# Attention's normalization moved into the transposes: a diagonal matrix in place of the identity, and values ahead of transposes in TensorE's order

## The chip, the cores and the metric

The kernel runs on one core of one Trainium2 chip. The metric is the device time of one execution in microseconds (us), lower is better. The engines are named as in the profile: PE (TensorE), DVE (VectorE), ACT (ScalarE), POOL (GpSimd), SP (SyncE, which issues DMAs).

## The reference, cut to what matters

Two layers over 512 latent and 256 context tokens of width 1024. Each layer is a mixer and a SwiGLU feed-forward network, with norms and modulation around both. The change touches the attention in both mixers.

```python
# layer 0, 8 query heads of width 64, 2 key/value heads; latent and context queries
p = softmax(concat([s_loc, s_ctx, sink_l], axis=-1))        # the sink is one more logit per head
o = p[..., :nk] @ v_band + p[..., nk:nk + L] @ v_ctx         # and has no value
# layer 1, 16 heads, latent queries only; s_loc has a relative-position bias
p = softmax(concat([s_loc, s_ctx], axis=-1))
o = p_loc @ v_seg + p_ctx @ v_ctx
```

A softmax row is exp(s - m) / sum. In both versions of the kernel the exps are taken first and the division comes later; the change is in where.

## The kernel before, in words

Each engine has one instruction stream, written out by hand, and waits on semaphores; `claim` and `read_by` on PE keep the eight PSUM banks apart. Around attention, products run in three passes of rounded operands (a high part and a low part, `h_hi` and `h_lo`), with weights split by ACT (`w_hi`, L830) and POOL (`w_lo`, L518).

Attention works in pairs of heads. Layer 0 has 24 pairs: six query tiles of 128 tokens, four pairs each. The tiles in order have 4, 5, 5, 4, 2 and 2 blocks of 128 keys. Layer 1 has 32 pairs of 4 blocks. Two pairs are a chunk, which fills one 128x256 output. For pair p:

- PE `scores(p)` (L1867) writes both heads' scores to PSUM.
- DVE `maximum(p)` (L1329, L1334, L1337) adds mask or bias, writes `prob` (two buffers, by p % 2) and the row maxima, and then the negated maximum `negm`.
- ACT `softmax(p)` (L930) takes the exps of the two heads in place, with the row sums in `rowsum`.
- PE `turns(p)` (L1888, fifth blocks L1895) transposes every 128x128 block of `prob` against the identity, head x = 0 into bank 4 and x = 1 into bank 5; fifth blocks go to bank 4 once it has been read.
- ACT `evacuate(p)` (L919, fifth blocks L922) copies x = 0, DVE `evacuate(p)` (L1347) copies x = 1.
- PE `values(p)` (L1923) multiplies with the values into bank 6 or 7.
- Per chunk: DVE inverts the row sums (L1356, L1365, L1368; in layer 0 with the sink's exp from ACT, L965); PE `norms` (L1935) spreads the inverses over the output's layout with four matmuls; ACT `inverse_rows` (L938) copies them to SBUF; DVE `normalize` (L1374) multiplies; ACT `high` (L945, L949) and DVE `low` (L1383, L1388) split the result into `h_hi` and `h_lo`.

PE's order in step p is scores(p), turns(p-1), values(p-2), and norms in odd steps. ACT's is evacuate(p-1), inverse rows, softmax(p), high. DVE's is maximum(p), the inverse, evacuate(p-1), normalize or low.

POOL takes no part in layer 0's attention. Just ahead of it POOL copies and splits the GLA heads' output (L732, L734), six tiles. In layer 1 POOL adds the relative bias and the mask for pair p (L781), once DVE has read that of pair p-1; in the first four steps it copies a mixed value tile (L792), and in steps 2, 4 and 6 it makes the low part of one weight unit of the output product (L518).

The output products `out0L` and `out1L` (L1716) begin when the last chunk's low part is there. The gate row `gate_b` for layer 1's post-norm is loaded by an ACT DMA during the query and key projection (`gate_load(act, 2)`, L1137).

```python
                for p in range(n_pairs + 2):                       # PE, before
                    if p == 0:
                        start(lambda: scores(0))
                    elif p < n_pairs:
                        scores(p)
                    if 1 <= p <= n_pairs:
                        turns(p - 1)
                    if p >= 2:
                        values(p - 2)
                        if p % 2 == 1:
                            norms(p // 2 - 1)
```

## Time and profile before

| | |
|---|---|
| Time, median of 3 runs (lowest to highest) | 1751.51 us (1749.96 to 1753.03) |
| The profiled execution's own time | 1752.69 us |
| Its span, first to last instruction | 1750.9 us |
| Mean granted PE clock | 0.987 |
| PE busy | 1667.4 us, 95% |
| DVE, ACT, POOL busy | 708.4, 644.1, 676.9 us |
| Layer 0's attention, first transposes to the output product | 275.3 to 358.2 us |
| Layer 1's attention, first transposes to the output product | 1201.7 to 1314.7 us |

Positions are microseconds from the start of the span. A row of the timeline has the start, the length, the engine, the line, the operation with its operands, the count of records merged, and in brackets the engine's idle time before it with what ended it. Matmul ends are modelled and matmuls overlap, so PE's progress is read from the starts.

### The profile page before, as it was taken

Reading aid. Unit: us, or ns where it says so; the run is one execution under the profiler, and the core shown is the slowest. Engines: PE = TensorE matmul, PEld = TensorE weight load, DVE = VectorE, ACT = ScalarE, POOL = GpSimd, SP = SyncE. Lnnn points to the kernel's source line nnn. Section 1 sums busy time; section 2 is a strip of 40 time slices with the busy share of each in tenths; the row PEclk is TensorE's granted clock in tenths of the full one; section 3 lists DMA queues with packets and bytes.
Section 4 is the critical chain, followed back from the end, with each engine's and each line's share of the span. In section 5 each row is a group of like instructions: output and inputs, shape, how many; then the busy total and the mean of one; then the engine's idle time right before and its main releaser. Section 6 shows DMA issues by size and latency. Waiting matters only on the chain.

```text
span 1750.9 us, 25757 instructions
## 1 busy us (share of the span) xinstructions
PE 1667.4 (95%) x10178; PEld 1387.9 (79%) x10178; DVE 708.4 (40%) x1121; ACT 644.1 (37%) x1120; POOL 676.9 (39%) x456
## 2 busy tenths in 40 slices
PE   5999998999999999999899999999999899999997
PEld 2868886777877888878899878877887788888886
DVE  3335456717588735402555420005771551011103
ACT  4242215727422122213555343235772522222222
POOL 2212222038554544443542043334443444444443
PEclk9999999999999999999999999999999899999999
DMA  8643111023466746533556645433002353333331
GB/s 325 212 150 99 42 25 49 2 73 108 145 193 193 230 143 188 167 91 109 145 169 183 193 117 113 92 94 101 2 2 60 100 165 95 105 90 98 96 98 69
DMA packets 210131, 207.17 MB, mean 118 GB/s; under 512 B 16454, under 2 KB 180828, under 8 KB 209756
## 3 DMA queue, kind: packets, MB, share of 16 engines
q1 hardware_dynamic: 197352, 165.53, 31.7%
q10 hardware_dynamic: 12660, 39.99, 7.4%
q8 instruction: 82, 1.34, 0.3%
q14 instruction: 37, 0.30, 0.1%
HBM read 203.37 MB, written 2.13 MB: 117 GB/s over the span
## 4 chain that ended last, share of the span: by engine, by line
PE 82%; DVE 5%; issue 4%; POOL 3%; ACT 3%; DMA 2%; SPq 0%; ACTq 0%; POOLq 0%; DVEq 0%
PE ps L1689 39%; PE ps L1716 29%; PE ps L1867 3%; PE ps L1923 3%; PE ps L1888 3%; POOL w_lo L518 3%; DMA mod_early<-in_w_mod 1%; ACT w_hi L830 1%; PE ps L1763 1%; PE ps L1802 1%; DVE xs L1278 1%; PE ps L1935 1%; PE ps L2051 1%; DVE full L1227 1%; DMA w_raw<-in_w_ffn_in 1%
## 5 line engine op out<-in xcount | busy, mean ns | idle before, releaser
L518 POOL TENSOR_TENSOR w_lo<-w_raw,w_hi 128x1024 fp32r<-128x1024 f32 (+1 forms) x223 | 557.5, 2502 | 896.3 <-ACT w_hi L830 896.1
L1689 PE MATMUL ps<-h_hi,w_hi 128*128 128x512 f32 (+1 forms) x1488 | 496.7, 352 | 11.7 <-POOL w_lo L518 8.0
L1689 PE MATMUL ps<-h_hi,w_lo 128*128 128x512 f32 (+1 forms) x1488 | 492.0, 349 | 0.0
L1689 PE MATMUL ps<-h_lo,w_hi 128*128 128x512 f32 (+1 forms) x1488 | 491.0, 348 | 0.0
L830 ACT ACTIVATE w_hi<-w_raw 128x1024 fp32r<-128x1024 f32 (+1 forms) x275 | 287.2, 1046 | 354.2 <-PE ps L1716 342.8
L1689 PEld LDWEIGHTS ps<-h_hi,w_hi 128*128 128x128 f32 x1488 | 270.0, 189 | 56.6 <-issue 20.2
L1689 PEld LDWEIGHTS ps<-h_hi,w_lo 128*128 128x128 f32 x1488 | 269.8, 189 | 36.2
L1689 PEld LDWEIGHTS ps<-h_lo,w_hi 128*128 128x128 f32 x1488 | 269.8, 189 | 36.0
L518 DVE TENSOR_TENSOR w_lo<-w_raw,w_hi 128x1024 fp32r<-128x1024 f32 x52 | 69.2, 1332 | 200.5 <-ACT w_hi L830 197.5
L1716 PE MATMUL ps<-w_hi,hid_hi 128*128 128x512 f32 x440 | 136.7, 392 | 8.0 <-ACT mod_row L842 4.2
L1297 DVE TENSOR_TENSOR hid_f<-silu_g,ps 128x512 f32<-128x512 f32 (+1 forms) x66 | 39.3, 595 | 255.3 <-PE ps L1689 254.9
L1716 PE MATMUL ps<-w_hi,hid_lo 128*128 128x512 f32 x440 | 136.1, 391 | 0.0
L1716 PE MATMUL ps<-w_lo,hid_hi 128*128 128x512 f32 x440 | 135.9, 390 | 0.0
L901 ACT ACTIVATE hid_hi<-hid_f 128x512 fp32r<-128x512 f32 (+1 forms) x66 | 37.0, 561 | 252.9 <-DVE hid_f L1297 252.9
L1716 PE MATMUL ps<-w_hi,h_hi 128*128 128x512 f32 (+1 forms) x352 | 106.4, 384 | 13.8 <-POOL w_lo L518 3.5
L1716 PE MATMUL ps<-w_lo,h_hi 128*128 128x512 f32 (+1 forms) x352 | 105.4, 382 | 0.0
L1716 PE MATMUL ps<-w_hi,h_lo 128*128 128x512 f32 (+1 forms) x352 | 104.8, 379 | 0.0
L1716 PEld LDWEIGHTS ps<-w_hi,hid_hi 128*128 128x128 f32 x440 | 82.7, 189 | 27.2 <-issue 10.3
L1716 PEld LDWEIGHTS ps<-w_lo,hid_hi 128*128 128x128 f32 x440 | 82.9, 188 | 17.4
L1716 PEld LDWEIGHTS ps<-w_hi,hid_lo 128*128 128x128 f32 x440 | 82.9, 188 | 17.3
L1716 PEld LDWEIGHTS ps<-w_hi,h_hi 128*128 128x128 f32 x352 | 66.5, 192 | 28.2 <-issue 7.1
L897 ACT ACTIVATE silu_g<-ps 128x512 f32<-128x512 f32 (+1 forms) x66 | 34.6, 524 | 145.8 <-PE ps L1689 145.6
(213 smaller groups left out, 1790.4 us busy)
## 6 DMA issues: line engine op xcount, KB each, us to landing
w_raw<-in_w_ffn_in SPq DMA_DIRECT2D x132, 512.0 KB, 3.8
w_raw<-in_w_ffn_out SPq DMA_DIRECT2D x66, 512.0 KB, 3.5
mod_raw<-in_w_mod ACTq DMA_DIRECT2D x42, 512.0 KB, 4.5
w_raw<-in_na_w_in SPq DMA_DIRECT2D x32, 512.0 KB, 3.7
mod_early<-in_w_mod SPq DMA_DIRECT2D x30, 512.0 KB, 9.0
full<-in_w_mod ACTq DMA_DIRECT2D x15, 512.0 KB, 4.9
w_raw<-in_ab_w_in SPq DMA_DIRECT2D x9, 512.0 KB, 4.6
w_raw<-in_ab_w_in SPq DMA_DIRECT2D x16, 256.0 KB, 3.8
```

What stands on the lines that cost most here:

```text
L518: eng.tensor_tensor(w_lo[:, u % RING, 0:width], w_raw[:, u % RAW, 0:width], w_hi[:, u % RING, 0:width].bitcast(F32), ALU.subtract).then_in ...
L830: act.activation(w_hi[:, u % RING, 0:width], w_raw[:, u % RAW, 0:width], ACT.Copy).then_inc(w_hi_done, 1)
L897: act.activation(silu_g[:, f % 2, 0:width], ps(2 * (f % 2), 0, width), ACT.Silu)\
L901: act.activation(hid_hi[:, j * width:(j + 1) * width], hid_f[:, f % 2, 0:width], ACT.Copy)\
L1227: dve.scalar_tensor_tensor(post_place(name, i), src, rs_post[:, n:n + 1], gate_b[:, lc, :], ALU.mult, ALU.mult).then_inc(post_n, 1)
L1278: dve.scalar_tensor_tensor(acc, mod_place(m), c, acc, ALU.mult, ALU.add).then_inc(mod_acc, 1)
L1297: dve.tensor_tensor(hid_f[:, f % 2, 0:width], silu_g[:, f % 2, 0:width], ps(2 * (f % 2) + 1, 0, width), ALU.mult).then_inc(ff_full, 1)
L1689: mm = pe.matmul(o[0], sta(x, o), mov(y, o), start=first and n == 0, stop=last and n == 2)
L1716: mm = pe.matmul(o, act(x, k, t), w[y][:, c:c + n], start=k == 0 and (x, y) == ("hi", "hi") and first_in_bank(name, i, c), stop=k == n_uni ...
L1867: mm = pe.matmul(ps(scores_bank(layer, p, x), at, at + width), q, kk[:, col:col + width], start=at % 512 == 0, stop=i == len(runs[x]) - 1, ...
L1888: mm = pe.transpose(ps(4 + x, j * P, (j + 1) * P), probs(p, x, j), ident[:])
L1923: mm = pe.matmul(ps(bank, at, at + P, 64 * x, 64 * x + 64), value_tile(p, x, j), turned_probs(layer, p)[:, x, j * P:(j + 1) * P], start=j ...
```

## The change

It does six things.

1. `turns` becomes a matmul of each block of `prob` with a diagonal matrix of the inverse row sums, one 128x128 diagonal per head, so that the transposed block comes out normalized. It waits for that diagonal once per pair.
2. POOL makes the diagonals, `scale(layer, p)`: a power of -1 on the two row sums, then the identity times the inverse, broadcast, 128x256. There is one buffer for them, so `scale(p)` also waits for the turns of p-1.
3. The sink becomes a column of `prob` in layer 0, written by POOL (`sink_column`), so that the exp's row sum holds it.
4. `norms`, `inverse_rows`, `normalize`, the shift and the inverse on DVE are gone; `high` and `low` read PSUM directly.
5. PE's order in step p becomes scores(p), values(p-2), turns(p-1). `prob` has three buffers, and `maximum(p)` waits for the turns of p-3.
6. `gate_load(act, 2)` moves behind layer 1's attention, since the third prob buffer takes `gate_b`'s place.

```diff
@@ POOL, ahead of feed(sp("out0C")), after the copies of the GLA output
+            feed(sp("out0L") + 1)
+            def sink_column(p):
+                f = PAIRS[0][p][2]
+                if p >= 3:
+                    pool.wait_ge(at_p, 2 * (p - 2))
+                pool.tensor_scalar(prob0[:, p % 3, :, 0:1].rearrange("p x n -> p (x n)"), sink[:, f:f + 5:4], 1.0 / SCALE,
+                                   None, ALU.mult).then_inc(at_sink, 1)
+            def scale(layer, p):
+                q = PAIR0[layer] + p
+                n = CHUNK0[layer] + p // 2
+                pool.wait_ge(at_p, 2 * (q + 1))
+                if p:
+                    pool.wait_ge(at_ta, q)
+                    pool.wait_ge(at_tb, q)
+                    if fifths(layer, p - 1):
+                        pool.wait_ge(at_t5, fifths(layer, p - 1))
+                rows, inv = (x[:, 2 * (p % 2):2 * (p % 2) + 2] for x in (rowsum[:, n % 2, :], sm[:, n % 2, 3, :]))
+                pool.tensor_tensor(inv, rows, one_hot[:, 34:36], ALU.pow).then_inc(at_rinv, 1)
+                pool.wait_ge(at_rinv, q + 1)
+                one = ident[:]
+                one = bass.AP(one.tensor, one.offset, [list(one.ap[0]), [0, 2], [1, P]])
+                pool.tensor_tensor(scale_of(layer), one, bcast(inv, P), ALU.mult).then_inc(at_scale, 1)
+            for p in range(3):
+                sink_column(p)
+            for p in range(len(PAIRS[0])):
+                scale(0, p)
+                if p + 3 < len(PAIRS[0]):
+                    sink_column(p + 3)
@@ POOL, layer 1, at the end of the loop over pairs that adds the bias
+                if p:
+                    scale(1, p - 1)
+            scale(1, len(PAIRS[1]) - 1)
@@ ACT attention
-                for p in range(n_pairs + 3):
+                for p in range(n_pairs + 2):
+                    if p % 2 == 1 and p >= 3:
+                        high((p - 3) // 2)
                     if 1 <= p <= n_pairs:
                         evacuate(p - 1)
-                    if p % 2 == 0 and p >= 4:
-                        inverse_rows(p // 2 - 2)
                     if p < n_pairs:
                         softmax(p)
@@ ACT
-                    if i == 6:
-                        gate_load(act, 2)
...
             attention(1, lambda: layer1_values("v1C", C_TILES))
+            act.wait_ge(at_p, 2 * (PAIR0[1] + len(PAIRS[1])))
+            act.wait_ge(at_ta, PAIR0[1] + len(PAIRS[1]))
+            act.wait_ge(at_tb, PAIR0[1] + len(PAIRS[1]))
+            gate_load(act, 2)
@@ DVE attention
-                for p in range(n_pairs + 4):
+                for p in range(n_pairs + 2):
                     if p < n_pairs:
                         maximum(p)
-                        if p % 2 == 1 and layer == 0:
-                            shift(p // 2)
-                    if p % 2 == 0 and 2 <= p <= n_pairs:
-                        inverse(p // 2 - 1)
+                    if p % 2 == 1 and p >= 3:
+                        low((p - 3) // 2)
                     if 1 <= p <= n_pairs:
                         evacuate(p - 1)
-                    if p % 2 == 0 and p >= 4 and p // 2 - 2 < n_pairs // 2:
-                        normalize(p // 2 - 2)
-                    if p % 2 == 1 and p >= 5:
-                        low(p // 2 - 2)
@@ PE attention
                 def turns(p):
                     n = s_cols(layer, p) // P
+                    pe.wait_ge(at_scale, q0 + p + 1)
                     for x in range(2):
-                        pe.wait_ge(at_p, 2 * (q0 + p) + x + 1)
                         claim(4 + x)
                         for j in range(min(n, 4)):
-                            mm = pe.transpose(ps(4 + x, j * P, (j + 1) * P), probs(p, x, j), ident[:])
+                            mm = pe.matmul(ps(4 + x, j * P, (j + 1) * P), probs(p, x, j), scale_of(layer)[:, x, :],
+                                           start=True, stop=True)
...
                     elif p < n_pairs:
                         scores(p)
+                    if 2 <= p <= n_pairs + 1:
+                        values(p - 2)
                     if 1 <= p <= n_pairs:
                         turns(p - 1)
-                    if p >= 2:
-                        values(p - 2)
-                        if p % 2 == 1:
-                            norms(p // 2 - 1)
```

## Rows read from the trace of the kernel before

**Rows 1.** The page: engines over the span, and the chain by engine.
```profile
PE 1667.4 (95%) x10178; PEld 1387.9 (79%) x10178; DVE 708.4 (40%) x1121; ACT 644.1 (37%) x1120; POOL 676.9 (39%) x456
...
PE 82%; DVE 5%; issue 4%; POOL 3%; ACT 3%; DMA 2%; SPq 0%; ACTq 0%; POOLq 0%; DVEq 0%
```

**Rows 2.** Timeline of layer 1's attention, two steps (start, length, engine, line, operation).
```profile
1228.26 1.09 PE L1888 MATMUL ps<-ident,prob 128*128 128x128 f32 x8
...
1228.95 0.60 ACT L919 ACTIVATE prob_t<-ps 128x512 f32<-128x512 f32 x1 [0.86 <-PE ps L1888]
...
1229.29 0.44 PE L1923 MATMUL ps<-prob_t,c_v 128*64 128x128 f32 x4
...
1229.45 0.38 ACT L938 ACTIVATE on<-ps 128x256 f32<-128x256 f32 x1
...
1230.24 0.72 ACT L930 ACTIVATE prob<-prob,negm 128x512 f32<-128x512 f32 x1 [0.41 <-DVE negm L1337]
...
1231.48 1.09 PE L1888 MATMUL ps<-ident,prob 128*128 128x128 f32 x8
...
1231.58 0.19 ACT L930 ACTIVATION_READ_ACCUMULATOR prob<-prob,negm 128x1 f32 x1
...
1235.14 1.09 PE L1888 MATMUL ps<-ident,prob 128*128 128x128 f32 x8
```

**Rows 3.** An fp32 matmul's records (timeline), and the transposes of layer 1 (groups by form).
```profile
195.12 1.95 PE L2051 MATMUL ps<-b_v,att_m 128*128 128x128 f32 x16
...
L1888 PE MATMUL ps<-ident,prob 128*128 128x128 f32 x256 | 36.0, 284 | 2.5 <-ACT prob L930 2.4
```

**Rows 4.** Groups by form on POOL (count, busy us, mean ns of one, idle before).
```profile
L781 POOL TENSOR_TENSOR bias_m<-rel,near_b 128x256 f32<-128x256 f32 x16 | 10.6, 682 | 25.5 <-DVE raw_max L1329 25.5
...
L792 POOL COPY x_res<-c_v 64x1024 f32<-64x1024 f32 x4 | 4.1, 1035 | 12.7 <-ACT c_v L1144 12.3
```

**Rows 5.** POOL's power, line 712 (min/median/max ns, first and last start).
```profile
L712 POOL TENSOR_TENSOR rs_pre<-ms_pre,half_neg x22: 550/551/1622, 15.1 to 1369.8; 128x1 f32<-128x1 f32 x22
...
L712 POOL TENSOR_TENSOR gla_rs<-gla_ms,half_neg x6: 1007/1010/1018, 200.1 to 265.4; 128x4 f32<-128x4 f32 x6
```

**Rows 6.** Timeline of ACT in layer 0, a step of five blocks.
```profile
299.82 0.60 ACT L919 ACTIVATE rope<-ps 128x512 f32<-128x512 f32 x1 [0.54 <-PE ps L1888]
...
301.23 0.82 ACT L930 ACTIVATE prob<-prob,negm 128x640 f32<-128x640 f32 x1
...
302.76 0.19 ACT L930 ACTIVATION_READ_ACCUMULATOR prob<-prob,negm 128x1 f32 x1
```

**Rows 7.** Groups by form in layer 0's attention: the exp of two blocks.
```profile
L930 ACT ACTIVATE prob<-prob,negm 128x256 f32<-128x256 f32 x16 | 8.0, 502 | 1.2 <-DVE negm L1334 0.9
```

**Rows 8.** Timeline at the start and the end of layer 0's attention.
```profile
275.34 1.97 PE L1888 MATMUL ps<-ident,prob 128*128 128x128 f32 x8 [0.89 <-ACT prob L930]
...
278.88 1.27 POOL L734 TENSOR_TENSOR h_lo<-b_o,h_hi 128x512 fp32r<-128x512 f32 x1
...
353.45 0.87 PE L1888 MATMUL ps<-ident,prob 128*128 128x128 f32 x4
...
358.22 0.70 PE L1716 MATMUL ps<-w_hi,h_hi 128*128 128x512 f32 x2 [2.24 <-DVE h_lo L1383]
```

**Rows 9.** Timeline at the start and the end of layer 1's attention.
```profile
1202.83 2.36 POOL L518 TENSOR_TENSOR w_lo<-w_raw,w_hi 128x1024 fp32r<-128x1024 f32 x1 [4.43 <-ACT w_hi L830]
...
1206.11 1.87 PE L1888 MATMUL ps<-ident,prob 128*128 128x128 f32 x8 [2.27 <-ACT prob L930]
...
1308.67 1.36 PE L1888 MATMUL ps<-ident,prob 128*128 128x128 f32 x8 [0.17 <-ACT prob L930]
...
1314.72 0.70 PE L1716 MATMUL ps<-w_hi,h_hi 128*128 128x512 f32 x2 [2.28 <-DVE h_lo L1388]
```

**Rows 10.** Windows (stretch, us, busy PE PEld DVE ACT POOL, PE clock, DMA share, GB/s).
```profile
275.00:281.00 6.00, 5.66 (x24) 4.33 (x24) 4.00 (x13) 3.69 (x11) 4.92 (x5) 0.50 0.46 133
840.00:860.00 20.00, 15.75 (x126) 15.03 (x125) 9.69 (x14) 10.98 (x18) 9.52 (x7) 1.00 0.46 134
```

More of the change, by code:

```diff
@@ L274, in build @@
         with ExitStack() as early:
-            sb("before", [P, D], scope=early)
+            prob1_c = sb("prob1_c", [P, 2, 4 * P], scope=early)
             rel = sb("rel", [P, 2, 8, BIAS_RUN], scope=early)
-            on1 = sb("on1", [P, 2 * P], scope=early)
+            scale1 = sb("scale1", [P, 2, P], scope=early)
         with ExitStack() as early:
@@ L338, in build @@
             a_q = sb("a_q", [P, 4, TOK], scope=s1)
+            with ExitStack() as s2:
+                prob0 = sb("prob0", [P, 3, 2, 1 + 5 * P], scope=s2)
             qg = sb("qg", [P, 4, TOK], scope=s1)
-            with ExitStack() as s2:
-                prob0 = sb("prob0", [P, 2, 2, 5 * P], scope=s2)
             kg = sb("kg", [P, 4, TOK], scope=s1)
@@ L624, in scores_bank, with prob_of, scale_of @@
             return 2 * x if layer == 0 else 2 * x + p % 2
-        def mixed_out(layer):
-            return full[:, 0:2, :].rearrange("p k n -> p (k n)") if layer == 0 else on1[:]
+        def prob_of(layer, p, x):
+            if layer == 0:
+                return prob0[:, p % 3, x]
+            return prob1_c[:, x] if p % 3 == 2 else prob1[:, p % 3, x]
+        def scale_of(layer):
+            return full[:, 0:2, :] if layer == 0 else scale1[:]
         block = ctx.enter_context(nc.Block())
@@ L911, in attention @@
                 pairs, q0, c0 = PAIRS[layer], PAIR0[layer], CHUNK0[layer]
-                prob = (prob0, prob1)[layer]
                 def evacuate(p):
@@ L961, in attention @@
                         meanwhile()
-                    if p % 2 == 1 and p < n_pairs and layer == 0:
-                        c = c0 + p // 2
-                        act.wait_ge(at_shift, c + 1)
-                        act.activation(sm[:, c % 2, 1, :], sm[:, c % 2, 0, :], ACT.Exp).then_inc(at_sink, 1)
-                    if p % 2 == 0 and p >= 4:
-                        high(p // 2 - 2)
             act.dma_start(x_res[:, 0:LT, :], a["x"][0].rearrange("(t p) d -> p t d", p=P)).then_inc(x_in, 16)
@@ L1310, in attention @@
                 pairs, q0, c0 = PAIRS[layer], PAIR0[layer], CHUNK0[layer]
-                prob = (prob0, prob1)[layer]
                 def maximum(p):
@@ L1316, in maximum @@
                     t, g, f = pairs[p]
[L1317 to L1321 removed]
+                    if p >= 3:
+                        dve.wait_ge(at_ta, q0 + p - 2)
+                        dve.wait_ge(at_tb, q0 + p - 2)
+                        if fifths(layer, p - 3):
+                            dve.wait_ge(at_t5, fifths(layer, p - 3))
                     for x in range(2):
@@ L1328, in maximum @@
                             added = bias_m[:, 2 * P * x:2 * P * x + n]
-                        dve.tensor_tensor_reduce(prob[:, s, x, 0:n], ps(scores_bank(layer, p, x), 0, n), added, 1.0,
+                        at = int(layer == 0)
+                        dve.tensor_tensor_reduce(prob_of(layer, p, x)[:, at:at + n], ps(scores_bank(layer, p, x), 0, n), added, 1.0,
                                                  -3.0e38, ALU.add, ALU.max, raw_max[:, s, x:x + 1]).then_inc(at_r, 1)
@@ L1773, in modulation_sum @@
                 claim(bank)
[L1774 removed]
+                pe.wait_ge(small_done, 5)
                 pe.wait_ge(mod_acc, sums_done(KT * (b + 1) - 1))
@@ L1848, in attention @@
                 pairs, q0, c0 = PAIRS[layer], PAIR0[layer], CHUNK0[layer]
-                prob = (prob0, prob1)[layer]
                 def scores(p):
@@ L1894, in turns @@
                         for x in range(2):
-                            mm = pe.transpose(ps(4, x * P, (x + 1) * P), probs(p, x, 4), ident[:])
+                            mm = pe.matmul(ps(4, x * P, (x + 1) * P), probs(p, x, 4), scale_of(layer)[:, x, :],
+                                           start=True, stop=True)
                         mm.then_inc(at_t5, 1)
@@ L1927, in values @@
                                 mm.then_inc(at_o, 1)
-                def norms(c):
-                    bank = 6 + (c0 + c) % 2
-                    pe.wait_ge(at_rinv, c0 + c + 1)
-                    for i in range(2):
-                        for x in range(2):
-                            r = sm[:, (c0 + c) % 2, 3, 2 * i + x:2 * i + x + 1]
-                            mm = pe.matmul(ps(bank, (2 + i) * P, (3 + i) * P, 64 * x, 64 * x + 64),
-                                           bass.AP(r.tensor, r.offset, [list(r.ap[0]), [0, 64]]), ident[:],
-                                           start=True, stop=True, skip_group_check=True)
-                            mm.then_inc(at_rr, 1)
-                    read_by((bank,), (at_on, c0 + c + 1))
+                    if p % 2 == 1:
+                        read_by((bank,), (at_lo, c0 + p // 2 + 1))
                 n_pairs = len(pairs)
```

56 lines of the change are left out of this document (12 added, 44 removed).

## The prediction

> **What bounds the kernel now.** The page comes first: its engine row and its chain [rows 1]. The reader is to see that PE is busy 95% of the span and holds 82% of the chain that ended last, so PE time is kernel time almost everywhere, and that the other engines, under 41% each, have room on average. An average says nothing of a stage, so the second view is the timeline of layer 1's attention, two steps of its steady part [rows 2]. PE works without a gap over 0.2 us: transposes at 1228.26, values at 1229.29, the next transposes at 1231.48, the ones after at 1235.14. A step without norms is 3.22 us, one with norms 3.66 us. The norms cost 0.44 us of PE per chunk and nothing else separates the two steps. ScalarE's evacuation, exps and sums go on beside this.
>
> **What is removed from PE.** Four norm matmuls per chunk of two pairs, 0.44 us each chunk [rows 2]. There are 16 chunks in layer 1 and 12 in layer 0: 7.0 + 5.3 = 12.3 us if PE stays the bound. With them go four DVE operations and two or three of ScalarE per chunk; they lie beside PE in the steady part and are priced at nothing, except at the two tails, below.
>
> **The transposes become products.** A transpose is one record of the trace: 8 per pair, 32 pairs, 256 records [rows 3]. They take 0.86 us per pair, 0.107 each, since values start 1.03 us after them of which 0.17 is issue. An fp32 matmul of the same full width, 128x128 on 128 columns, is two records: the eight of one tile are 16 records, whose starts run over 1.95 - 0.27 = 1.68 us in 15 intervals, 0.111 apart [rows 3]. So I take 0.222 us for each product with the diagonal, against 0.107. A pair of four blocks goes from 0.86 to 1.78 us, +0.92. By PE alone a layer 1 step is 3.22 + 0.92 = 4.14 us against a mean of 3.44: already slower, norms or not. The ends are 0.107 (should the product be one record) and, upward, 0.25.
>
> The rule that speaks against this more strongly: the Trainium skill, "TensorE: Matmul & The Clock Gate", section Terms, calls the transpose mode 4x faster for FP32 than what it replaces. By it a product would take four times 0.107, 0.43 us. The fp32 rows of this kernel say 0.222, and the sum goes by them.
>
> **The order closes a loop.** This is the main term. Transposes of p-1 now wait for the diagonal of p-1 (both exps, then two POOL operations), and ScalarE does evacuate(p-1), then softmax(p), in that order, while evacuate(p-1) waits for the transposes of p-1. So each step contains one full round: transposes(p-1), evacuation, two exps, POOL, transposes(p). Its length, from rows 2 for four blocks:
> - transposes to the evacuation's start: 0.69 now (1228.26 to 1228.95), with four records of half x=0. Eight records add 4 x 0.111 + 0.03: 1.16.
> - evacuation, until ScalarE's next operation: 0.50 (1228.95 to 1229.45).
> - both exps and their sums: 1230.24 to 1231.58 + 0.19 = 1.53.
> - POOL: the power and the diagonal of 128x256. The diagonal's nearest row is the bias add of the same size, 0.68 [rows 4]. The power of 128x1 is 0.55 and of 128x4 1.01 [rows 5], so 128x2 by the line between them is 0.70. Three hand-overs are some 0.25, by the 0.10 between the modelled end of the fourth transpose (0.32 + 0.27 after the first's start) and the evacuation. Together 1.63.
>
> The sum is 4.82 us per step, more than PE's 4.14, so the loop sets the step and not PE. Before, the same round needed no POOL, one exp fewer ahead of the first half, and eight records fewer: it fitted into 3.22 us. DVE is not in it: its maxima of p start when scores(p) are out, which the new order leaves early, and evacuate of x=1 ends about 2.75 us into the round, ahead of the values.
>
> For layer 0 the blocks vary. Five blocks: the evacuation's start to the softmax is 1.41 (299.82 to 301.23), because the fifth blocks are turned between; their two transposes become four records, +0.22; the exps take 302.76 + 0.19 - 301.23 = 1.72 [rows 6]. Round: 1.16 + 1.63 + 1.72 + 1.63 = 6.14 us. Two blocks: an exp is 0.50 [rows 7], the pair of them with sums 1.10, the evacuation half of the above, the first half four records (0.70): 0.70 + 0.28 + 1.10 + 1.63 = 3.71 us.
>
> **Layer 0's sum.** From the first transposes to the last there are 23 rounds. Three of four blocks 14.5, the change to five 5.0, seven of five 43.0, the change back 5.95, three of four 14.5, the change to two 4.4, seven of two 26.0: 113.2 us. Now it is 353.45 - 275.34 = 78.1 [rows 8]. So +35.1. The start: POOL reaches its sink columns only after its copies of GLA output, which end at 278.88 + 1.27 = 280.15 [rows 8], and the softmax waits for them. First transposes: 280.15 + 0.3 + 1.53 + 1.63 = 283.6 against 275.34, +8.3. Tail: the last transposes (0.89), DVE's evacuation, eight value records, high, low, first product: about 3.5 against 4.77, -1.3.
>
> **Layer 1's sum.** POOL's queue ahead of diagonal 1: w_lo to 1202.83 + 2.36 = 1205.19, two bias adds 1.36, the copy of v_mix 1.04 [rows 4, 9], then 1.63: 1209.2 against 1206.11, +3.1. The same queue (2.36 + 1.36 + 1.63, a little more where a bias comes in four adds) outlasts two later rounds by about 0.7 each, +1.4. Thirty rounds of 4.82 are 144.6 against 1308.67 - 1206.11 = 102.6 [rows 9], +42.0. Tail: 1.78 for the products, then evacuation, values, high, low: 5.4 against 6.05, -0.6.
>
> **The clock.** While POOL holds the start PE idles; now after such an idle the granted clock was 0.50, the 1.2 GHz level, for 275 to 281 [rows 10]. At it a half's eight records take 0.9 us more. I add 2 us for two rounds in layer 0, 0.9 in layer 1 and 1 for the stage of two blocks, where PE will be busy under half the time. In the rest PE idles about 1 us a round; a stretch with PE busy 15.75 of 20 us kept 1.00 [rows 10].
>
> **Other edits.** The load of gate 2 moves behind layer 1's attention; its reader is the post-norm, which has the whole output product ahead of it and so hides it (uncovered, one load would be late once). A third prob buffer loosens maximum(p), which bound nothing. The sink column adds one column to 128x640. POOL's sink operations stand behind scale(p), inside the round's slack. POOL's prefetched w_lo of the output product is as far as ScalarE allows, as now. All nothing.
>
> Total: layer 0 +35.1 + 8.3 - 1.3 + 3 = +45.1; layer 1 +3.1 + 1.4 + 42.0 - 0.6 + 0.9 = +46.8. Together +92. The profiled execution took 1752.69 us, 1.2 above the median of 1751.51; against the median that is 1843 us.
>
> **Rivals.**
> 1. PE's own sum binds, because POOL or the hand-overs are quicker than I price, or ScalarE overlaps more. A round then is near PE's: 0.65 less over 54 rounds, -35: 1808. For it: 4.14 and 4.82 are close, and a power of 0.55 takes 0.15 off. Against: both POOL operations have rows of their kind. 15%.
> 2. The clock does not hold in layer 0. At 1.2 GHz a round of five blocks would be PE's doubled sum, some 9.4 us; for half of layer 0's rounds that is about +25: 1868. For it: idle of 1 to 1.6 us in every round, never seen here in a row. Against: at the low clock PE has no idle left, and rows 10. 12%.
> 3. The product costs four times a transpose. The first half adds 0.8 us to each round, and layer 1 becomes PE's, near 6.0: about +56 more, 1900. Rows 3 speak against it. The Trainium skill's 4x would give this. 3%.
> 4. Not slower: the products run as one record each and POOL's two operations hide, the norms' 12.3 us go, the start costs 8.3 + 3.1 and the tails give 1.9: about -3, 1749. It decides where the round falls under 3.22 us. Without POOL it would be 0.69 + 0.50 + 1.53 = 2.72, so POOL would have to take 0.5; the power alone has 0.55 at the least. 3%. The 5% left lie between it and rival 1, 2 of them near the time of now.
>
> **Range and chances.** The forecast has 62%, with a range of its own of 1825 to 1865: the power's ends are -0.15 and +0.31 on 54 rounds (-8, +17), the diagonal -0.05 to +0.1, the hand-overs 0.1 either way. Rivals 1 and 2 with theirs bring it to 1800 to 1880. A measurement of this kernel can tell about 0.2% from no change. Rival 4 and those 2 make faster 0.02 and same 0.03; all else is slower, 0.95.
>
> **What would show it.** In the profile after: 16 matmul records per pair of four blocks where 8 transposes were, some 0.11 apart; layer 1's transposes repeating every 4.8 us, five-block ones every 6.1; PE waiting in them for POOL's diagonal, 0.5 to 1.3 us a step; the power near 0.70 and the diagonal near 0.68; ScalarE waiting for PE before each evacuation; the first transposes of layer 0 near 283.6. Steps near 4.1 us with no wait for POOL would make rival 1 right, a granted clock under 0.9 over the attention stages rival 2, and steps under 3.4 us the whole reading wrong.

## The result and the profile after

The changed kernel takes 1839.44 us, the median of 4 runs (1837.74 to 1843.27), against 1752.06 (1749.96 to 1753.03) for the kernel before in the same session: 1.0508 times as long, with a 95% interval of 1.0491 to 1.0525. The forecast was 1843 us. The profiled execution spans 1837.9 us, 87.0 more than before. Line numbers below are those of the changed kernel: its transposes are now the products of L1885 (fifth blocks L1893), scores L1864, values L1922, the products of the output projection L1714; POOL's power is L762 and its diagonal L766.

The page of the kernel after, engines and chain, against [rows 1]:

```profile
PE 1707.9 (93%) x10386; PEld 1430.9 (78%) x10386; DVE 703.9 (38%) x1041; ACT 631.7 (34%) x1080; POOL 755.0 (41%) x593
...
PE 76%; POOL 8%; ACT 6%; issue 5%; DVE 4%; DMA 1%; SPq 0%; ACTq 0%; POOLq 0%; DVEq 0%
```

PE is busy 40.5 us more, which is less than half of what the span grew by. The rest shows in the chain: PE falls from 82% to 76%, POOL rises from 3% to 8% and ScalarE from 3% to 6%. Engines that had little part in the chain now carry more of it.

A steady round of layer 1, from the timeline (start, length, engine, line, operation, count, idle before and releaser), against [rows 2]:

```profile
1292.57 2.05 PE L1885 MATMUL ps<-scale,prob 128*128 128x128 f32 x16 [0.48 <-POOL scale L766]
...
1293.77 0.60 ACT L959 ACTIVATE prob_t<-ps 128x512 f32<-128x512 f32 x1 [2.73 <-PE ps L1885]
1294.26 0.71 ACT L972 ACTIVATE prob<-prob,negm 128x512 f32<-128x512 f32 x1
...
1295.58 0.19 ACT L972 ACTIVATION_READ_ACCUMULATOR prob<-prob,negm 128x1 f32 x1
...
1295.85 0.71 POOL L762 TENSOR_TENSOR sm<-rowsum,one_hot 128x2 f32<-128x2 f32 x1 [1.76 <-ACT prob L972]
...
1296.63 0.61 POOL L766 TENSOR_TENSOR scale<-ident,sm 128x256 f32<-128x256 f32 x1
...
1297.30 2.05 PE L1885 MATMUL ps<-scale,prob 128*128 128x128 f32 x16 [0.48 <-POOL scale L766]
```

The reader can walk round it: products to evacuation 1.20, evacuation to exps 0.49, exps and sums 1.51, a hand-over of 0.08, the power and its own hand-over 0.78, the diagonal and the last hand-over 0.67. That is 4.73 us, and no engine is busy all through it: PE waits 0.48, ScalarE 2.73, POOL 1.76. This is how a loop looks in a timeline. Each engine has a gap, each gap names the next engine, and the lengths of one turn add up to the step.

The waits of layer 1's attention, 1250 to 1395 (engine and line, waited for, us in total, times, longest), and POOL's groups over the whole kernel (count, busy us, mean ns of one, idle before), against [rows 4, 5]:

```profile
ACT prob_t L959 <- PE ps L1885: 60.3, 30, 4.5
...
POOL sm L762 <- ACT prob L972: 32.7, 18, 2.1
...
PE ps L1885 <- POOL scale L766: 17.6, 30, 2.1
...
POOL sm L762 <- ACT prob_c L972: 16.3, 9, 2.1
```

```profile
L762 POOL TENSOR_TENSOR sm<-rowsum,one_hot 128x2 f32<-128x2 f32 x56 | 39.7, 710 | 130.7 <-ACT prob L972 114.1 <-ACT prob_c L972 16.3
L766 POOL TENSOR_TENSOR scale<-ident,sm 128x256 f32<-128x256 f32 x32 | 19.7, 614 | 2.5
```

PE waits for the diagonal in all 30 rounds of this stretch, though only for 17.6 us in all. A saving of POOL's time alone would win at most these 17.6 us in this stretch; below that PE's own sum takes over.

In layer 0 a step of five blocks, a step of two, the start and the end, against [rows 6, 8]; the last two rows are the start of layer 1's second round and its end, against [rows 9]:

```profile
277.45 1.26 POOL L741 TENSOR_TENSOR h_lo<-b_o,h_hi 128x512 fp32r<-128x512 f32 x1
278.80 0.82 POOL L749 TENSOR_SCALAR prob<-sink 128x2 f32<-128x2 f32 x3
279.10 1.28 ACT L972 ACT_TABLE_LOAD   x1 [11.64 <-POOL prob L749]
280.40 0.72 ACT L972 ACTIVATE prob<-prob,negm 128x513 f32<-128x513 f32 x1
...
317.05 2.05 PE L1885 MATMUL ps<-full,prob 128*128 128x128 f32 x16 [1.05 <-POOL full L766]
...
323.19 2.05 PE L1885 MATMUL ps<-full,prob 128*128 128x128 f32 x16 [1.05 <-POOL full L766]
...
379.57 1.16 PE L1885 MATMUL ps<-full,prob 128*128 128x128 f32 x8 [1.28 <-POOL full L766]
...
383.21 1.16 PE L1885 MATMUL ps<-full,prob 128*128 128x128 f32 x8 [1.02 <-POOL full L766]
...
402.19 1.19 PE L1714 MATMUL ps<-w_hi,h_hi 128*128 128x512 f32 x2 [1.50 <-DVE h_lo L1387]
...
1252.51 3.45 PE L1885 MATMUL ps<-scale,prob 128*128 128x128 f32 x16 [2.11 <-POOL scale L766]
...
1401.96 0.93 PE L1714 MATMUL ps<-w_hi,h_hi 128*128 128x512 f32 x2 [1.37 <-DVE h_lo L1392]
```

Five blocks take 6.14 us and two blocks 3.64. The first products of layer 0 start at 283.47 and those of the last pair at 397.78, so its rounds take 114.3 us where 78.1 were. The output product of layer 0 starts 43.97 us later than before. Layer 1's attention runs from its first products at 1245.08 to 1401.96, 156.9 us against 113.0 (1201.68 to 1314.72): 43.8 more. The two make 87.8, so everything outside the two stages, the moved load of the gate row included, gives back 0.8 to the 87.0 of the span.

Windows of the kernel after (stretch, us, busy PE PEld DVE ACT POOL, PE clock, DMA share, GB/s), against [rows 10]:

```profile
275.00:281.00 6.00, 0.00 (x0) 0.00 (x0) 0.00 (x0) 1.88 (x2) 4.22 (x7) 0.50 0.27 84
303.00:347.00 44.00, 36.59 (x380) 31.07 (x376) 21.68 (x51) 19.98 (x48) 11.53 (x22) 1.00 0.01 1
370.00:398.00 28.00, 18.26 (x159) 12.96 (x159) 12.19 (x47) 11.79 (x43) 11.67 (x21) 1.00 0.00 1
1250.00:1395.00 145.00, 126.14 (x1284) 110.44 (x1282) 80.75 (x210) 66.99 (x182) 90.05 (x170) 0.99 0.04 12
```

The gaps of 0.5 to 1.3 us in every round leave the granted clock at 0.99 to 1.00, the 2.4 GHz level, even among the steps of two blocks, where PE is busy 18.3 of 28 us.

### The profile page after: what moved, and what is told of

The parts are those of the page before. It is cut to its first block, busy times and chain, and to the rows that moved or that the text cites. A ratio compares the mean times of both kernels' runs of the same rounds, so it can differ in the third digit from the quotient of the medians.

```text
span 1837.9 us, 26165 instructions
## 1 busy us (share of the span) xinstructions
PE 1707.9 (93%) x10386; PEld 1430.9 (78%) x10386; DVE 703.9 (38%) x1041; ACT 631.7 (34%) x1080; POOL 755.0 (41%) x593
## 4 chain that ended last, share of the span: by engine, by line
PE 76%; POOL 8%; ACT 6%; issue 5%; DVE 4%; DMA 1%; SPq 0%; ACTq 0%; POOLq 0%; DVEq 0%
PE ps L1687 39%; PE ps L1714 28%; PE ps L1885 4%; ACT prob L972 3%; POOL w_lo L517 2%; POOL sm L762 2%; DMA mod_early<-in_w_mod 1%; POOL scale L766 1%; ACT w_hi L871 1%; PE ps L1800 1%; PE ps L1761 1%; DVE xs L1310 1%; POOL full L766 1%; ACT prob_c L972 1%; PE ps L2038 1%
## 5 line engine op out<-in xcount | busy, mean ns | idle before, releaser
L1714 PE MATMUL ps<-w_hi,hid_hi 128*128 128x512 f32 x440 | 136.0, 390 | 8.0 <-ACT mod_row L883 4.3
L1714 PE MATMUL ps<-w_lo,hid_hi 128*128 128x512 f32 x440 | 135.5, 389 | 0.0
L1714 PE MATMUL ps<-w_hi,hid_lo 128*128 128x512 f32 x440 | 135.5, 389 | 0.0
L1714 PE MATMUL ps<-w_hi,h_hi 128*128 128x512 f32 (+1 forms) x352 | 107.0, 386 | 11.9 <-POOL w_lo L517 3.2
L1714 PE MATMUL ps<-w_lo,h_hi 128*128 128x512 f32 (+1 forms) x352 | 105.5, 382 | 0.0
L1714 PE MATMUL ps<-w_hi,h_lo 128*128 128x512 f32 (+1 forms) x352 | 105.2, 381 | 0.0
L1714 PEld LDWEIGHTS ps<-w_hi,hid_hi 128*128 128x128 f32 x440 | 82.1, 188 | 27.0 <-issue 10.3
L1714 PEld LDWEIGHTS ps<-w_lo,hid_hi 128*128 128x128 f32 x440 | 82.6, 188 | 17.3
L1714 PEld LDWEIGHTS ps<-w_hi,hid_lo 128*128 128x128 f32 x440 | 82.6, 188 | 17.2
L762 POOL TENSOR_TENSOR sm<-rowsum,one_hot 128x2 f32<-128x2 f32 x56 | 39.7, 710 | 130.7 <-ACT prob L972 114.1
L1714 PEld LDWEIGHTS ps<-w_hi,h_hi 128*128 128x128 f32 x352 | 66.9, 193 | 26.2 <-issue 5.6
```

The lines of the kernel that those rows point to most:

```text
L762: pool.tensor_tensor(inv, rows, one_hot[:, 34:36], ALU.pow).then_inc(at_rinv, 1)
L1714: mm = pe.matmul(o, act(x, k, t), w[y][:, c:c + n], start=k == 0 and (x, y) == ("hi", "hi") and first_in_bank(name, i, c), stop=k == n_uni ...
```

## The experiments

The theory going in: two costs, the products on PE (+0.9 a pair) and a loop through ScalarE and POOL, the longer of which sets the step. The rivals: PE's sum alone, a costlier product, and PE's new order. Each run is compared with the kernel before in its own session, whose median lies between 1748.06 and 1752.06, so a difference of 2 or 3 us between medians of two sessions says nothing by itself; where one matters, the stages are read from the traces. The runs stand in the order of the questions.

**Is it PE's order?** `e1_old_pe_order` turns pair p-1 before it takes the values of p-2, as the kernel before did.

```
@@ ACT: high(c) behind softmax(p); DVE: low(c) behind evacuate(p-1)
@@ PE attention
-                    if 2 <= p <= n_pairs + 1:
-                        values(p - 2)
                     if 1 <= p <= n_pairs:
                         turns(p - 1)
+                    if 2 <= p <= n_pairs + 1:
+                        values(p - 2)
```

> The changed kernel with TensorE's old order (transposes of p-1 ahead of values of p-2); ACT's high and DVE's low go behind the evacuation, since they wait for those values. Theory (the round transposes, ACT evacuation, two exps, POOL power and diagonal, transposes sets the step, and values are not in it): layer 1 stays at 4.73 us a step, five blocks at 6.14, total 1839 within 4 us. Rival (TensorE's new order is what opens the gap): steps fall towards TensorE's own sum of 4.15 us, total about 1805.

Measured: 1836.8 us, ratio 1.0493 (1.0476 to 1.0511). Its products in layer 1 stand at 1262.03 and 1266.75, 4.72 us apart. The medians differ by 2.6 us, which is not clear of the noise (87.4 and 86.2 over the kernel before of each session), and the step is the same in either order. The loop does not need PE's new order. That it needs the other two things, products that wait for POOL and a ScalarE that evacuates p-1 before it takes the exps of p, is for the runs below.

**What do the products cost by themselves?** `e3_before_with_products` is the kernel before with each transpose written as an fp32 matmul with the identity.

```
-   mm = pe.transpose(ps(4 + x, j * P, (j + 1) * P), probs(p, x, j), ident[:])
+   mm = pe.matmul(ps(4 + x, j * P, (j + 1) * P), probs(p, x, j), ident[:], start=True, stop=True)
```

> The kernel before with one part of the change alone: each transpose is an fp32 matmul with the identity. Theory (0.222 us for a product against 0.107 for a transpose, and TensorE is the bound): +0.92 us for each pair of four blocks in layer 1 (+29), in layer 0 +0.92 x 8, +1.15 x 8, +0.46 x 8 (+20, a little less where ACT is waited for): total about 1799. Rival 1 (a product is one record like a transpose): 1752. Rival 2 (a product costs four transposes, 0.43 us): +2.6 us a pair, total above 1880.

Measured: 1792.61 us in a single execution, 42 above the 1750.61 of the kernel before beside it. PE's timeline in layer 1:

```profile
1264.23 2.05 PE L1888 MATMUL ps<-ident,prob 128*128 128x128 f32 x16
...
1268.31 2.05 PE L1888 MATMUL ps<-ident,prob 128*128 128x128 f32 x16
...
1272.83 2.05 PE L1888 MATMUL ps<-ident,prob 128*128 128x128 f32 x16
```

The products are followed by the next operation 1.98 us after their start, where transposes take 1.03 [rows 2]: 0.95 a pair, against 0.92 predicted. The steps are 4.08 us, and 4.52 with norms, where the same pairs took 3.13 and 3.56 before (transposes at 1241.92, 1245.05 and 1248.61; their scores are shorter than those of [rows 2]), and none waits. The Trainium skill ("TensorE: Matmul & The Clock Gate", Terms) has the transpose mode 4x faster for FP32, and doesn't say against what; with the 0.17 of issue taken off both, the rows say 1.81 to 0.86, 2.1 times, and the measurement decides.

**And POOL's wait by itself?** `e4_transposes_wait_for_pool` is the kernel after with plain transposes that still wait for the diagonal. It leaves the normalization out.

```
-   mm = pe.matmul(ps(4 + x, j * P, (j + 1) * P), probs(p, x, j), scale_of(layer)[:, x, :], start=True, stop=True)
+   mm = pe.transpose(ps(4 + x, j * P, (j + 1) * P), probs(p, x, j), ident[:])
```

> The changed kernel with plain transposes against the identity in place of the products, still waiting for POOL's diagonal; the normalization is left out of the output. Theory (only the first half's four extra records lie in the round, the other half's beside it): layer 1 4.73 to 4.26 us, five blocks 6.14 to 5.45, two blocks 3.64 to 3.42: total about 1814. Rival (TensorE's sum is the bound, so all of the doubling comes back): -0.92 us a pair, total about 1791.

Measured: 1812.03 us in a single execution. PE's timeline in layer 1:

```profile
1265.74 1.09 PE L1885 MATMUL ps<-ident,prob 128*128 128x128 f32 x8
...
1269.96 1.09 PE L1885 MATMUL ps<-ident,prob 128*128 128x128 f32 x8 [0.93 <-POOL scale L766]
```

4.22 us a step: the loop without the four products of its first half, 4.73 less some 0.5. PE now idles 0.93 of it.

**The other two corners.** `e8_products_without_pool` keeps after's order and products, but multiplies by the identity and waits for the exps alone. `e11_neither_product_nor_pool` is the same with plain transposes in place of the last line below. Both leave the normalization out.

```
@@ POOL
-                scale(0, p)
...
@@ PE turns
-                    pe.wait_ge(at_scale, q0 + p + 1)
+                    pe.wait_ge(at_p, 2 * (q0 + p + 1))
...
+                            mm = pe.matmul(ps(4 + x, j * P, (j + 1) * P), probs(p, x, j), ident[:], start=True, stop=True)
```

> The changed kernel without POOL's power and diagonal: products with the identity that wait for the two exps alone; the normalization is left out of the output. Theory (POOL's two operations with their hand-overs are 1.5 us of each round, and without them TensorE's own sum binds): layer 1 at 4.2 us, five blocks at about 5.0, two blocks at 2.1 to 2.3, total about 1797. Rival (the round is set by ACT and DVE): total 1825 or more.

> The kernel after with plain transposes, and with POOL's power and diagonal out of the step: the transposes wait for the two exps alone. The normalization is left out, for this is the fourth corner beside the two runs that have the products without POOL (1793.25) and POOL's wait without the products (1812.03). Theory: PE is the bound again, in layer 1 at 3.12 to 3.22 us a step with no step longer, since the norms are out of it: by the 0.44 us of PE per chunk that is -12.3 us against the kernel before; the start of layer 0 keeps its wait for the sink columns (+5 to +6.6), the tails give 1 to 2. Together 1742 to 1746. The corner then says that the products alone cost 49 and POOL's wait alone 68, and that both together cost less than their sum, because one hides in the other. Rival: the two kernels' difference by products is the 41 us measured on the kernel before, so this run gives 1793.25 - 41 = 1752, and taking the norms off PE was worth next to nothing, because ScalarE's order (evacuation, then both exps, now with both exps ahead of every transpose) makes a round as long as PE's sum: then PE waits for prob in each step and steps exceed 3.22 us.

Measured: 1793.25 us in a single execution for the first, with steps of 4.18 and 4.08 us in layer 1 that wait for nothing, 5.02 for five blocks and 2.38 for two. The second takes 1748.23 (10 runs), ratio 0.9986 (0.9975 to 0.9996), which fell between the two numbers expected of it. Its mechanism is the theory's, with steps of 3.12 us and no wait (1249.81, 1252.93, 1256.05 for the transposes of layer 1), so the rival's loop is not there. Its size is not: the start of layer 0 cost more than was allowed for, as PE's and ScalarE's rows there show:

```profile
279.71 1.28 ACT L968 ACT_TABLE_LOAD   x1 [11.63 <-POOL prob L749]
...
282.58 1.97 PE L1881 MATMUL ps<-ident,prob 128*128 128x128 f32 x8 [8.51 <-ACT prob L968]
```

The transposes start 7.2 us later than in [rows 8], in a stage that itself started 0.8 us earlier, so the wait for the sink columns costs 8.0. What taking the norms off PE gives back is therefore about 11.5, the shorter tails with it: 3.5 net and these 8.0. The traces agree: from the first transposes to the output product layer 0 takes 77.9 us instead of 82.9, layer 1 106.3 instead of 113.0. The four corners together:

```
                          transposes   products
waiting for the exps      1748.2       1793.3
waiting for POOL          1812.0       1839.4
```

Products alone cost 45 us, POOL's wait alone 64, both 91 and not 109: some 18 us of either hide in the other. Two of the four are single executions, and each is of another session. The same two stages in the traces, from the first transposes to the output product, give 46, 63 and 91, so the picture holds. This is also why the change can't be mended by making one of the two cheap.

**Can ScalarE's order open the loop?** `e2_softmax_first` lets ScalarE take the exps of p before it evacuates p-1.

```
@@ ACT attention
                 for p in range(n_pairs + 2):
+                    if p < n_pairs:
+                        softmax(p)
                     if p % 2 == 1 and p >= 3:
                         high((p - 3) // 2)
                     if 1 <= p <= n_pairs:
                         evacuate(p - 1)
-                    if p < n_pairs:
-                        softmax(p)
```

> The changed kernel with one order turned on ACT: softmax(p) ahead of evacuate(p-1), so that the exps of p no longer wait for the transposes of p-1. Theory: the round is cut, and TensorE's own sum is next: layer 1 4.73 to 4.15 us a step (-17 us over 30 steps), five blocks 6.14 to about 5.0 (-9), four blocks in layer 0 to 4.0 (-5), two blocks 3.64 to about 2.6, where the single diagonal buffer binds (-8): total about 1800. Rival (POOL's two operations and their hand-overs set the step by themselves): total stays at 1839.

Measured: 1827.39 us, ratio 1.0442 (1.0427 to 1.0458). A miss by 27 us, by the stages in the trace half of it in layer 1 and half in layer 0. PE's timeline and one wait of 1250 to 1380:

```profile
1286.70 0.44 PE L1922 MATMUL ps<-prob_t,c_v 128*64 128x128 f32 x4 [0.82 <-DVE prob_t L1379]
...
1287.72 2.05 PE L1885 MATMUL ps<-scale,prob 128*128 128x128 f32 x16
...
1291.90 2.05 PE L1885 MATMUL ps<-scale,prob 128*128 128x128 f32 x16
...
1296.98 2.05 PE L1885 MATMUL ps<-scale,prob_c 128*128 128x128 f32 x16
```

```profile
DVE h_lo L1392 <- ACT h_hi L985: 26.8, 14, 1.9
```

Every second step is the 4.18 us expected; the others take 5.08. In those ScalarE's high() now stands behind the exps, DVE's low() waits for it, and DVE's own evacuation, which the values need, is queued behind low(). What wasn't counted in layer 1 was the queue behind the instruction that waits. `e5_softmax_first_evacuate_next` puts both evacuations ahead of high() and low().

```
@@ ACT: softmax(p), evacuate(p-1), high
@@ DVE
                         maximum(p)
-                    if p % 2 == 1 and p >= 3:
-                        low((p - 3) // 2)
                     if 1 <= p <= n_pairs:
                         evacuate(p - 1)
+                    if p % 2 == 1 and p >= 3:
+                        low((p - 3) // 2)
```

> The changed kernel with ACT's order softmax(p), evacuate(p-1), high, and DVE's order maximum(p), evacuate(p-1), low. With the softmax first but high and low ahead of the evacuations (e2) layer 1's steps alternated between 4.18 and 5.08 us. Theory (in the long steps DVE's evacuation stood behind low, which waited for ACT's high, which waited for the exps): both steps come to 4.18 us, TensorE's own sum, total about 1814. Rival (something else of odd steps costs 0.9 us): total stays at 1827.

Measured: 1813.4 us, ratio 1.0361 (1.0339 to 1.0383). The step of layer 1:

```profile
1271.51 2.05 PE L1885 MATMUL ps<-scale,prob 128*128 128x128 f32 x16
...
1275.73 1.49 PE L1885 MATMUL ps<-scale,prob_c 128*128 128x128 f32 x11
```

4.22 us with no gap on PE: in layer 1 the loop is open and PE's own sum binds, as rival 1 would have had it. In layer 0 it is not open for five blocks:

```profile
315.52 2.05 PE L1885 MATMUL ps<-full,prob 128*128 128x128 f32 x16
...
318.59 0.71 PE L1893 MATMUL ps<-full,prob 128*128 128x128 f32 x4 [1.02 <-ACT rope L959]
...
321.77 2.05 PE L1885 MATMUL ps<-full,prob 128*128 128x128 f32 x16
```

A step is 6.25 us there, where the changed kernel has 6.14, the first run with the exps first was expected to have 5.0, and the corner without POOL has 5.02. The fifth blocks go to bank 4 and wait for ScalarE's evacuation of it, which now stands behind both exps, and the scores of the next pair stand behind the fifth blocks: the new order opens one loop and closes another. Two blocks take 2.86 (371.03 to 385.33, five steps) against 3.64. The forecast of 1814 came true with this unseen: it lies 14 us above the sum of the run before, and no term of it is named for the difference.

So some 26 of the change's 87 us are ScalarE's order (with DVE's): 10.3 in layer 0 and 16.1 in layer 1 by the two stages in the traces. The change's scheme stays 3.6% slower even so, since the products alone are worth 45 and the five-block steps some 10 more (1.23 each over the corner without POOL, for eight pairs).

**The start of layer 0.** `e7_sinks_before_copies` has POOL write the sink columns first and spread its six copies between the rounds.

```
@@ POOL
             for p in range(3):
                 sink_column(p)
+            for t in range(3):
+                mixed_copy(t)
             for p in range(len(PAIRS[0])):
                 scale(0, p)
...
+                if p + 3 < NT:
+                    mixed_copy(p + 3)
```

> The changed kernel with POOL's sink columns and three of six GLA copies ahead of layer 0's attention, the other copies one each behind diagonals 0 to 2, and ACT waiting for the sink ahead of the maximum. Theory (POOL's copies ahead of the sink hold the start of layer 0's attention, with the exp table load behind that wait): the first transposes 6 us earlier, total about 1832. Rival (the start is hidden, or the copies are only moved): total stays at 1839.

Measured: 1833.21 us (1828.52 to 1836.69), ratio 1.0476 (1.0442 to 1.0509): near the 1832 expected. But against the kernel before of its session it is 85 us longer, the changed kernel 87, and its four runs lie 8 us apart, so the total doesn't settle it. The trace does:

```profile
272.38 1.28 ACT L977 ACT_TABLE_LOAD   x1 [5.23 <-DVE negm L1371]
...
276.74 3.78 PE L1890 MATMUL ps<-full,prob 128*128 128x128 f32 x16 [2.84 <-POOL full L767]
```

The first products start 6.7 us earlier than in the changed kernel (276.74 against 283.47, 0.3 of it because the stage started earlier), and layer 0's output product 6.9 earlier (395.27). So the start's wait is real time, some 6.5 us of it. Part stays, for the table load is still in the way.

**Can the norms leave PE without a product?** The corner without either cost says that plain transposes with the norms off PE are not slower than before. `e6_normalize_in_place` scales prob before plain transposes: DVE takes the reciprocal, POOL multiplies both halves by it, and PE turns p-2 and takes the values of p-3, so that the scaling has a step of its own.

```
@@ POOL
-                pool.tensor_tensor(scale_of(layer), one, bcast(inv, P), ALU.mult).then_inc(at_scale, 1)
+                for x in range(2):
+                    head = 2 * (p % 2) + x
+                    w = prob_of(layer, p, x)[:, at:at + n]
+                    last = pool.tensor_scalar(w, w, sm[:, c % 2, 3, head:head + 1], None, ALU.mult)
+                last.then_inc(at_scale, 1)
@@ PE: scores(p), turns(p-2), values(p-3)
```

> Another place for the division: plain transposes against the identity; DVE takes the reciprocals between its two maxima; POOL multiplies prob in place by them, two operations of 128x512; transposes of p-2 and values of p-3 in step p (three prob buffers do for it), so that the exps and POOL have a step more; the sink columns go ahead of the GLA copies on POOL. Theory (nothing of the round is left on TensorE's path and transposes stay at 0.107 us): the kernel before less the norms' 12.3 us and about 1 us of tails: about 1738, layer 1 at 3.22 us in every step. Rival (POOL, with bias 1.6 and products 1.2 us in each step of 3.22, becomes the bound or DVE waits for it): layer 1 at 3.4 to 3.7 us, total 1745 to 1760.

Measured: 1811.63 us, ratio 1.0349 (1.0328 to 1.037). A miss by 74 us: the rival came true, beyond its own range of 1745 to 1760. POOL's group and the window of layer 1 (columns as above):

```profile
L761 POOL TENSOR_SCALAR prob_c<-prob_c,sm 128x512 f32<-128x512 f32 x20 | 31.1, 1565 | 0.0
```

```profile
1215.00:1370.00 155.00, 105.82 (x1046) 87.30 (x1045) 88.51 (x246) 72.67 (x186) 151.79 (x177) 0.92 0.04 11
```

POOL is busy 151.8 of 155 us: it is the bound, and layer 1's steps are 4.65 us, 1.35 to 1.46 of them PE's wait for POOL. The Trainium skill ("GPSIMD Engine Reference", 4.1 Engine selection) calls POOL's one-input operations roughly line-rate and its two-input ones about 2x slower than VectorE's. Here the one-input form is the slow one: 1565 ns, where the two-input form of the next run takes 1042; the measurement decides.

`e9_in_place_act_and_pool` halves POOL's part: ScalarE scales x=0 by a copy with a scale, POOL x=1 by a tensor-tensor multiply that reads the same column again and again.

```
@@ ACT
+                    act.activation(w, w, ACT.Copy, scale=sm[:, c % 2, 3, 2 * (p % 2):2 * (p % 2) + 1]).then_inc(at_scaled, 1)
@@ POOL
+                inv = bass.AP(inv.tensor, inv.offset, [list(inv.ap[0]), [0, n]])
+                pool.tensor_tensor(w, w, inv, ALU.mult).then_inc(at_scale, 1)
```

> As e6, in place of POOL's two scalings by a per-row scalar, which took 1.57 us for 128x512 and held POOL for 3.1 us of each 4.6 us step: ACT scales head x=0 (a Copy with a scale, 0.50 us of ACT by the evacuation of the same size) and POOL head x=1 as a product of two tensors, 1.27 us by its subtraction of the same size. Theory (POOL's load of bias and scaling sets e6's step, not the pipeline): POOL comes to 1.6 + 1.3 = 2.9 us a step, layer 1 to 3.22 to 3.4 us, total 1737 to 1744, under the kernel before. Rival (the deeper pipeline itself costs, or POOL at 90% of a step is still the bound): layer 1 at 3.6 us or more, total 1752 or more.

Measured: 1747.42 us (11 runs), ratio 0.998 (0.9971 to 0.9989); 4 us under the kernel before beside it and 3 us above what was expected. Its groups by form:

```profile
L763 POOL TENSOR_TENSOR prob<-prob,sm 128x512 f32<-128x512 f32 x30 | 31.2, 1042 | 13.2 <-DVE sm L1358 13.2
L982 ACT ACTIVATE prob<-prob,sm 128x512 f32<-128x512 f32 x30 | 21.5, 715 | 1.1 <-DVE sm L1358 1.1
```

The steady steps are the 3.22 us of the theory (1226.58, 1229.80, 1233.02) and 3.12 further on, without a wait. The excess is at the start of layer 1's attention, where PE waits 1.58 us for POOL (1213.31) and 2.24 for DVE (1222.24) and the granted clock was 0.72 (1202 to 1214).

`e10_in_place_act_and_dve` gives x=1 to DVE, behind its maxima, and leaves POOL out.

```
@@ DVE
+                    dve.tensor_scalar(w, w, sm[:, c % 2, 3, head:head + 1], None, ALU.mult).then_inc(at_scale, 1)
@@ POOL
-                scale(0, p)
```

> As e9, with head x=1 scaled by DVE behind its maximum (0.4 us, by the 0.75 us of its 128x1024 scaling) and POOL out of it. Theory: DVE comes to about 3.05 us and ACT to 2.7 us a step, both under TensorE's 3.22, so layer 1 runs at 3.22 us in every step, layer 0 as before without norms: total about 1738, 12 us under the kernel before. Rival (DVE's queue is too full, or waits for POOL's bias adds where both read SBUF): layer 1 at 3.4 us or more, total 1744 or more.

Measured: 1741.28 us (1738.87 to 1743.2), ratio 0.9941 (0.9929 to 0.9954): 0.6% under the kernel before (10.1 us under the 1751.39 beside it), and 3 us above the forecast for it. PE's timeline in layer 1, the group of DVE's scaling, the end of layer 1, and the same stage in a window:

```profile
1250.47 1.19 PE L1897 MATMUL ps<-ident,prob 128*128 128x128 f32 x8
...
1253.68 1.09 PE L1897 MATMUL ps<-ident,prob 128*128 128x128 f32 x8
...
1304.13 0.70 PE L1726 MATMUL ps<-w_hi,h_hi 128*128 128x512 f32 x2 [1.37 <-DVE h_lo L1400]
```

```profile
L1348 DVE TENSOR_SCALAR prob<-prob,sm 128x512 f32<-128x512 f32 x30 | 21.2, 708 | 0.0
```

```profile
1250.00:1290.00 40.00, 40.00 (x440) 33.37 (x438) 38.77 (x114) 36.34 (x91) 20.62 (x46) 1.00 0.01 2
```

Steps are 3.1 to 3.2 us with PE busy 40 of 40, where every second one was 3.66 [rows 2], or 3.55 in this stretch of the kernel before (1251.73 to 1255.28). The price is that DVE (38.8) and ScalarE (36.3) are nearly full as well: there is little more to be had this way. From the scores of the second pair to the output product, layer 1's attention takes 110.0 us (1194.17 to 1304.13) against 114.1 (1200.62 to 1314.72), and layer 0's 80.3 (272.98 to 353.26) against 84.9 (273.32 to 358.22). These are 8.7 of the 13.1 us between the spans (1737.8 against 1750.9); the other 4.4 lie where the two kernels are the same: 0.3 ahead of layer 0's attention, 1.5 between the two (842.4 against 840.9) and 2.5 behind layer 1's (436.2 against 433.7), where the granted clock of the first 85 us was 0.96 against 0.92. That last part goes with the clock and is not shown to belong to the edit.

## Why the prediction was right

Right in sign, in size to 3.6 us, and in mechanism, step by step:

- *Four norm matmuls leave PE, 12.3 us.* About 11.5, from the corner without product and wait, the shorter tails with it.
- *A product at 0.222 against 0.107, +0.92 a pair.* 0.95, in the kernel before with products alone. Sixteen records a pair, as forecast.
- *The round at 4.82, and 6.14 and 3.71 in layer 0.* 4.73, 6.14 and 3.64. The power was put at 0.70 and is 0.71, the diagonal at 0.68 and is 0.614. A row of the same size but with another input (the bias add) was 0.07 too long; that is most of the 0.09.
- *"The order closes a loop."* The heading doesn't say whose order; the text under it names ScalarE's, evacuation before exps, together with the wait for the diagonal, and the runs bear that out. With PE's old order the step is the same 4.72; without POOL's wait it is 4.18; with the exps first and DVE's queue put right it is 4.2, PE's own sum. For five blocks that last exchange doesn't open it (6.25).
- *Layer 0's start +8.3, to 283.6.* 283.47, but two errors hide in this: the exp's table load of 1.28 us was not priced, and the stage started 1.4 us earlier than before. That they cancel is luck.
- *Layer 0's rounds 113.2 and 2 for the clock.* 114.3. *Its tail -1.3.* -0.4: the last products wait for the diagonal too, and the output product then begins 4.41 us after them, against 4.77. The granted clock was 0.56 there (398 to 404).
- *Layer 1: start +3.1, rounds +44.3 with the queue and the clock, tail -0.6.* +3.0, +41.5 and -0.7. The rounds' 2.8 too many are 0.09 in each of 30.
- *The clock, 1 us in the stage of two blocks.* Not needed: 1.00 there.

The sum is +87.8 by these parts against +92. Rival 1 (PE's sum binds, 1808) needed ScalarE to overlap more; it didn't here, and a kernel in which it does takes 1813, with PE's sum binding in layer 1 only. Rival 2 fell with the windows. Rival 3 fell with the products of the kernel before: 42 us, where four transposes' price would have given over 100. (By its own terms PE's step there is 5.8 us, 3.22 less 0.86 plus eight times 0.43, not "near 6.0".) Rival 4 had no footing, POOL's pair of operations being 1.32 us. The third prob buffer had no run of its own; the moved load of the gate row is among what is outside the two stages, 0.8 us in all.

## What to carry to other kernels

When an operand of a frequent step gets a new producer, write out the round from that step to itself, engine by engine, with the order in each queue: here it was 0.6 us over PE's sum, and an exchange of entries in ScalarE's and DVE's queues was worth some 26 us. Do it for every shape of the step: the exchange that opened the loop for four blocks left the step of five as long as it was. Two added costs that lie partly beside each other neither add up nor vanish (45 and 64 made 91), so measure each alone before mending either. And when work is to leave a full engine, scale the data where it already lies, with whichever engine has a slot in the step, before adding a product: the same division of rows cost 87 us as a product with a diagonal, 45 of them for the products alone, and gave 10 as two elementwise operations, 9 of them in the two attention stages.

## What the runs showed that was not expected

- A multiply by one value per row on POOL takes 1565 ns for 128x512 as a tensor-scalar operation, 1042 ns as a tensor-tensor operation that reads the column over and over, 716 ns on ScalarE. On DVE it takes 478 ns in layer 0 and 782 to 834 (means of two groups) in layer 1; why it is slower there was not tested.
- With a second wait ahead of the first exp, that exp's table load moved into the path. In the kernel before, with one wait, it ran while ScalarE waited for the maxima, and the exp started at 274.48:

```profile
269.27 1.28 ACT L930 ACT_TABLE_LOAD   x1 [0.40 <-ACT tri L884]
```

  With the sink columns' semaphore added it started only when both waits were over (279.10), 1.28 us, and putting that wait ahead of the one for the maxima didn't free it (272.38). The Trainium skill ("ScalarE: Activation LUTs", What ACT_TABLE_LOAD costs) has the same 1283 ns, and a drain of about 1380 ns behind it that no row here shows: the exp starts 1.30 after the load.
- Idle time in every round did not lower the granted clock here: it stayed at 1.00 with 1 us of it in 6.14 and with 1.35 in 4.65 (POOL as the bound, 1310 to 1350). The mean of 0.92 over that kernel's window of 155 us comes from its first part, 0.74 from 1215 to 1235, where PE was busy 8.9 of 20 us.
